# Attention by pairs of heads and modulation slabs by pairs, in a two-layer diffusion block

## The reference

```python
mod = silu(c) @ w_mod[layer] + b_mod[layer]        # 6 x 1024; the same for the context with c_ctx
hx = modulate(rms_norm(x, norm1_g), sh1, sc1)      # hc likewise
mx, mc = token_mixers(hx @ w_in, hc @ w_in, ...)   # GQA with 8 heads over 2 key heads, neighbourhood
                                                   # attention with 4 heads, pooling; gates, output projection
x = x + g1 * mx
hx = modulate(rms_norm(x, norm2_g), sh2, sc2)
x = x + g2 * (swiglu(h) if layer == 0 else moe_swiglu(hx))   # dense, then 2 of 8 experts
```

## Time and profile before

| stage | from | to |
|---|---|---|
| start: eight slabs, norm | 0 | 51.7 |
| projection, layer 0 | 51.7 | 155.5 |
| attention, pooling, layer 0 | 155.5 | 342.2 |
| merge, output projection, norm | 342.2 | 599.4 |
| feed-forward, norm of layer 1 | 599.4 | 1019.8 |
| projection, layer 1 | 1019.8 | 1100.0 |
| attention, pooling, layer 1 | 1100.0 | 1163.5 |
| merge, output projection, norm, router | 1163.5 | 1334.1 |
| experts, last norm | 1334.1 | 2379.4 |

### The profile page before, as it was taken

One profiled execution on the slowest core, in us unless ns is written; L12 is line 12 of the kernel. 1 busy time (PEld: TensorE's weight loads), 2 busy tenths in 40 slices (PEclk: granted clock), 3 DMA queues, 4 the chain that ended last, 5 costly groups with the idle time before them and its releaser, 6 DMA issues.

```text
span 2379.4 us, 27429 instructions
## 1 busy us (share of the span) xinstructions
PE 2286.7 (96%) x10670; PEld 1646.3 (69%) x10671; DVE 1159.3 (49%) x1372; ACT 1053.5 (44%) x1148; POOL 1287.2 (54%) x464
## 2 busy tenths in 40 slices
PE   6999999999999999899999899999999999999996
PEld 3875457664677878777797667677777777676774
DVE  3133421123101010335522687787878787878775
ACT  3222232202321222243431477666666666766664
POOL 2300013301443445440240599989898998898994
PEclk8999999999999999989999799999999999999998
DMA  7313442122233322231144699999999999999992
GB/s 279 109 54 124 148 173 89 71 89 106 89 136 141 109 93 80 80 124 36 56 193 158 266 364 344 348 341 350 340 345 344 352 357 336 352 342 347 347 346 101
DMA packets 69642, 503.17 MB, mean 211 GB/s; under 512 B 7744, under 2 KB 7872, under 8 KB 9088
## 3 DMA queue, kind: packets, MB, share of 16 engines
q1 hardware_dynamic: 68976, 497.91, 56.1%
q0 software_dynamic: 528, 3.41, 0.4%
HBM read 500.24 MB, written 1.05 MB: 211 GB/s over the span
## 4 chain that ended last, share of the span: by engine, by line
PE 50%; POOL 34%; issue 11%; ACT 2%; DVE 1%; DMA 1%; POOLq 0%; ACTq 0%; DVEq 0%; SPq 0%
POOL moe_lo L443 33%; PE bank L702 14%; PE bank L687 10%; PE bank L689 9%; PE bank L688 9%; PE pv_bank L702 2%; PE bank L853 2%; PE turned L872 1%; ACT H_NEW L1250 1%; DMA slab<-in_w_mod 1%; PE bank L857 1%; DMA moe_slab<-in_moe_up 0%; DVE SQ_SUM L1627 0%; PE bank L800 0%; POOL w_lo L413 0%
## 5 line engine op out<-in xcount | busy, mean ns | idle before, releaser
L443 POOL TENSOR_TENSOR moe_lo<-moe_slab,moe_hi 128x512 fp32r<-128x512 f32 x336 | 921.8, 2769 | 180.4 <-ACT moe_hi L1437 179.0
L443 DVE TENSOR_TENSOR moe_lo<-moe_slab,moe_hi 128x1536 fp32r<-128x1536 f32 x336 | 692.3, 2065 | 177.6 <-ACT moe_hi L1437 175.1
L413 POOL TENSOR_TENSOR w_lo<-slab,w_hi 128x2048 fp32r<-128x2048 f32 (+2 forms) x72 | 304.1, 4225 | 802.4 <-ACT w_hi L1214 802.3
L1437 ACT ACTIVATE moe_hi<-moe_slab 128x2048 fp32r<-128x2048 f32 x336 | 629.2, 1906 | 0.0
L687 PE MATMUL bank<-moe_hi,HE_HI 128*96 128x512 f32 x896 | 361.1, 403 | 9.0 <-issue 5.3
L689 PE MATMUL bank<-moe_hi,HE_LO 128*96 128x512 f32 x896 | 353.9, 395 | 0.0
L688 PE MATMUL bank<-moe_lo,HE_HI 128*96 128x512 f32 x896 | 352.7, 394 | 0.0
L687 PE MATMUL bank<-H_HI,w_hi 128*128 128x512 f32 (+1 forms) x880 | 326.5, 371 | 15.5 <-POOL H_LO L599 14.9
L688 PE MATMUL bank<-H_LO,w_hi 128*128 128x512 f32 (+1 forms) x880 | 319.8, 363 | 0.0
L689 PE MATMUL bank<-H_HI,w_lo 128*128 128x512 f32 (+1 forms) x880 | 319.6, 363 | 0.0
L1214 ACT ACTIVATE w_hi<-slab 128x2048 fp32r<-128x2048 f32 (+1 forms) x72 | 135.5, 1884 | 173.6 <-PE bank L689 114.0
(11 more groups left out here) (190 smaller groups left out, 2530.8 us busy)
## 6 DMA issues: line engine op xcount, KB each, us to landing
moe_slab<-in_moe_up SPq DMA_DIRECT2D x224, 1024.0 KB, 4.8
moe_slab<-in_moe_w SPq DMA_DIRECT2D x112, 1024.0 KB, 4.9
slab<-in_w_mod SPq DMA_DIRECT2D x48, 1024.0 KB, 4.8
slab<-in_w_in SPq DMA_DIRECT2D x38, 1024.0 KB, 4.8
slab<-in_ffn_w SPq DMA_DIRECT2D x30, 1024.0 KB, 4.8
slab<-in_w_proj SPq DMA_DIRECT2D x8, 1024.0 KB, 6.9
slab<-in_w_out SPq DMA_DIRECT2D x8, 1024.0 KB, 4.8
slab<-in_ffn_w SPq DMA_DIRECT2D x4, 768.0 KB, 4.2
```

The lines of the kernel that those rows point to most:

```text
L413: engine.tensor_tensor(lo, raw, hi.bitcast(F32), ALU.subtract).then_inc(done, 1)
L443: engine.tensor_tensor(moe_lo[n][:, blocks, :], moe_slab[k % MOE_RING][:, blocks, :], moe_hi[n][:, blocks, :].bitcast(F32), ALU.subtract). ...
L1437: af(moe_hi[k % MOE_SPLIT][:], moe_slab[k % MOE_RING][:], ACT.Copy).then_inc(moe_hi_ready, 1)
```

## The change

Heads go in pairs: a pair is the two heads that share a chunk of Y. Their scores are issued alternately from the two halves of the partitions of QK (or BQ), to different banks; their values go to the two halves of `pv_bank`, which ScalarE copies once for both. PT holds four heads' transposed probabilities instead of two. Latent and context pairs alternate in layer 0. TensorE's order is scores of the next pair (first query half), turn of head 0, values of the pair before, scores (second half), a pair of slabs, turn of head 1.

Slabs go in pairs: the sixteen matmuls of two slabs go in turn to four groups of 32 output partitions, the even and the odd eighths of the sum for each of two slabs. VectorE copies all 128 partitions. `turned_mod`, after two pairs, is four matmuls against a constant `fold` (128 x 4) that add the two halves of the sum and bring features to partitions. Pairs 0 to 3 (slabs 0 to 7) stand at the start, 4 to 15 in layer 0's attention, 16 to 21 (slabs 32 to 43) in layer 1's attention, 22 and 23 in the last norm. The second norm of layer 0, the feed-forward and the first norm of layer 1 have none.

```diff
@@ lists
-MOD_AT_START, MOD_IN_ATTENTION, MOD_IN_FFN = range(8), range(8, 32), range(34, 42)
-
-MOD_IN_NORM = {(0, 1): (), (0, 2): (32, 33), (1, 1): (42, 43), (1, 2): (44, 45, 46, 47)}
+MOD_PAIRS = 24
+MOD_AT_START = range(4)
...
+def attention_pairs(layer):
+    streams = (LAT, CTX) if layer == 0 else (LAT,)
+    return [(b, j, s) for b, n in (("A", 4), ("B", 2)) for j in range(n) for s in streams]
...
-    return [(b, h, s) for b, n in (("A", 8), ("B", 4)) for s in streams for h in range(n)]
+    return [(b, j, g, s) for b, j, s in attention_pairs(layer) for g in range(2)]
+MOD_IN_ATTENTION = (range(4, 16), range(16, 22))
+MOD_IN_NORM = (22, 23)
@@ TensorE
-            def mod(n):
...
-                filled(chain(out[32 * q:32 * q + 32, 0:256],
-                             [(small["cond"][:, 32 * k:32 * k + 32], w[:, k, :]) for k in range(DC)]), ("mod", n))
-                if q == 3:
-                    key = ("turned_mod", n // 4)
-                    out = fill(key)
-                    if n == 3:
-                        pe.wait_ge(consts_in, 16)
-                    for back in range(4):
-                        wait_taken(pe, ("mod", n - back))
+            def mod(i):
+                w, out = [slab(("mod", 2 * i + n))[0] for n in range(2)], fill(("mod", i))
+                for k in range(DC):
+                    for n in range(2):
+                        q = 2 * n + k % 2
+                        ins = mm(out[32 * q:32 * q + 32, 0:256], small["cond"][:, 32 * k:32 * k + 32], w[n][:, k, :],
+                                 start=k < 2, stop=k >= DC - 2)
+                filled(ins, ("mod", i))
+            def turned_mod(g):
+                out = fill(("turned_mod", g))
+                if g == 0:
+                    pe.wait_ge(consts_in, 16)
+                for q in range(2):
+                    wait_taken(pe, ("mod", 2 * g + q))
                     for m in range(2):
-                        ins = nc.tensor.transpose(out[:, P * m:P * m + P], small["modrow"][:, P * m:P * m + P], ident)
-                    filled(ins, key)
+                        row = 512 * (g % 2) + 256 * q + P * m
+                        ins = mm(out[:, 8 * q + 4 * m:8 * q + 4 * m + 4], small["modrow"][:, row:row + P], const("fold"),
+                                 start=True, stop=True)
+                filled(ins, ("turned_mod", g))
@@ TensorE, attention
+                    outs = [fill(("score", layer, 2 * p + g, t)) for g in range(2)]
+                        for g in range(2):
+                            lhs = q[half[g], c_lat + P * t:c_lat + P * t + P]
+                            filled(mm(outs[g][:], lhs, keys[g][half[g], :], start=True, stop=True),
+                                   ("score", layer, 2 * p + g, t))
...
-                    ins = chain(pv_bank[p0:p0 + HD, 0:S],
-                                [(V[:, t, vcol:vcol + HD], PT[:, u % 2, t, :]) for t in range(tiles)])
+                    for t in range(tiles):
+                        for g in range(2):
+                            ins = mm(pv_bank[HD * g:HD * g + HD, 0:S], V[:, t, cols[g]:cols[g] + HD],
+                                     PT[:, (2 * p + g) % 4, t, :], start=t == 0, stop=t == tiles - 1)
                     ins.then_inc(pv_full[layer], 1)
 
-                scores(0)
-                scores(1)
-                for u in range(len(units)):
-                    if u + 2 < len(units):
-                        scores(u + 2)
-                    if u:
-                        values(u - 1)
-                    turn(u)
-                    if layer == 0:
-                        mod(MOD_IN_ATTENTION[u])
-                values(len(units) - 1)
+                scores(0, 0)
+                scores(0, 1)
+                for p in range(len(pairs)):
+                    if p and p % 2 == 0:
+                        turned_mod(MOD_IN_ATTENTION[layer][p - 1] // 2)
+                    scores(p + 1, 0)
+                    turn(2 * p)
+                    if p:
+                        values(p - 1)
+                    scores(p + 1, 1)
+                    mod(MOD_IN_ATTENTION[layer][p])
+                    turn(2 * p + 1)
+                values(len(pairs) - 1)
+                turned_mod(MOD_IN_ATTENTION[layer][-1] // 2)
@@ ScalarE, attention
+                for p in range(len(pairs)):
+                    exps(2 * p + 1)
+                    turned_out(2 * p)
+                    if p:
+                        result(p - 1)
+                    if p + 1 < len(pairs):
+                        exps(2 * p + 2)
+                    turned_out(2 * p + 1)
@@ VectorE
+            def mod(i):
+                row = 256 * (i % 4)
+                wait_full(dve, ("mod", i))
...
@@ VectorE, attention
+                for p in range(pairs):
+                    normalise(2 * p)
+                    normalise(2 * p + 1)
+                    turned_out(2 * p)
+                    if p and p % 2 == 0:
+                        turned_mod(mods[p - 1] // 2)
+                    if p + 1 < pairs:
+                        maxima(2 * p + 2)
+                    mod(mods[p])
+                    turned_out(2 * p + 1)
+                    if p + 1 < pairs:
+                        maxima(2 * p + 3)
```

More of the change, by code:

```diff
@@ L113, in norm @@
             slabs.extend([("w1", 0, 0), ("w3", 0, 0)])
-        for n in MOD_IN_NORM[key]:
-            mod(n)
-    for n in MOD_AT_START:
-        mod(n)
+        if key == (1, 2):
+            for i in MOD_IN_NORM:
+                mod(i)
+            turned_mod(11)
+    for i in MOD_AT_START:
+        mod(i)
+        if i == 2:
+            turned_mod(0)
+    turned_mod(1)
     for layer in range(DEPTH):
@@ L130, in schedule, with scores @@
         fills.extend(("in", layer, ("u", m)) for m in range(layer, 2))
-        units = attention_units(layer)
-        for u in range(2):
-            fills.extend(("score", layer, u, q) for q in range(2 if units[u][2] == LAT else 1))
-        for u in range(len(units)):
-            if u + 2 < len(units):
-                fills.extend(("score", layer, u + 2, q) for q in range(2 if units[u + 2][2] == LAT else 1))
-            if layer == 0:
-                mod(MOD_IN_ATTENTION[u])
+        pairs = attention_pairs(layer)
+        def scores(p, t):
+            if p < len(pairs) and (pairs[p][2] == LAT or t == 0):
+                fills.extend(("score", layer, 2 * p + g, t) for g in range(2))
+        scores(0, 0)
[7 more added lines that the diff above has]
+        turned_mod(MOD_IN_ATTENTION[layer][-1] // 2)
         fills.extend(("pool", layer, p) for p in range(2))
@@ L156, in schedule @@
                     fills.extend([("w1", part, s, 0), ("w1", part, s, 1), ("w3", part, s, 0), ("w3", part, s, 1)])
-                    if later:
-                        mod(later.pop(0))
                 for j in range(4):
@@ L161, in schedule @@
                     fills.extend(("down", part, j, m) for m in range(2))
-                    if later:
-                        mod(later.pop(0))
-            assert not later
     fills.append(("logit",))
@@ L181, in last_fill @@
     if kind == "mod":
-        return slab
+        return ("mod", slab[1] // 2)
     if kind == "in":
@@ L874, in turn, with values @@
                     ins.then_inc(turned_full[layer], 1)
-                def values(u):
-                    branch, h, stream = units[u]
-                    _, p0, _, vcol, _ = place(branch, h)
-                    pe.wait_ge(turned_out_act[layer], u + 1)
-                    pe.wait_ge(turned_out_dve[layer], u + 1)
-                    if u == 0:
+                def values(p):
+                    branch, j, stream = pairs[p]
+                    cols = place(branch, j)[2]
+                    pe.wait_ge(turned_out_act[layer], 2 * p + 2)
+                    pe.wait_ge(turned_out_dve[layer], 2 * p + 2)
+                    if p == 0:
                         for name in (("av", 0), ("av", 1), ("bv", 0), ("bv", 1)):
@@ L1306, in attention @@
             def attention(layer):
[L1307 removed]
+                pairs = attention_pairs(layer)
                 def exps(u):
[L1310 removed]
+                    stream = pairs[u // 2][2]
                     act.wait_ge(nm_ready[layer], u + 1)
@@ L1635, in residuals @@
                         sum_squares(norm_key, *x_range(layer), c - 1)
-                    if c % 2 and later and norm_key != (layer, 2):
-                        mod(later.pop(0))
                 if norm_key:
@@ L1964, in expert @@
                     add_quarter(n, 4 * i + n + 1)
-            later = list(MOD_IN_FFN)
             v.memset(small["cond"][:], 0.0).then_inc(cond_zeroed, 1)
             dve.wait_ge(vecs_in, 16)
-            for n in MOD_AT_START:
-                if n == 4:
+            for i in MOD_AT_START:
+                if i == 2:
                     for c in range(1, DC):
                         sum_squares((0, 1), 0, T, c)
-                mod(n)
+                mod(i)
```

(3 more changed lines are left out.)

175 lines of the change are left out of this document (79 added, 96 removed).

## The result

The changed kernel takes 2307.8 us (median of 4 runs) beside 2380.5 us of the kernel before on the same chip: a ratio of 0.9691, 95% interval 0.9678 to 0.9703. It is faster by 73 us. The forecast was 2292, so the gain is 16 us short of it, inside the range. The profiled execution spans 2309.8 us, 17.9 above the 2291.9 of the sum. It is the slowest of the four; the fastest took 2302.7 us, at a mean granted clock of 0.966 instead of 0.959.

The account below looks back on a forecast made before the run. No single engine bounds the whole span; halving TensorE's work leaves a three-engine round trip pacing layer 0's attention. Terms +5.2 − 69.9 − 2.7 − 28.2 − 3.1 + 10.8 + 0.4 = −87.5 give 2292 us, range 2278 to 2320.

Parts of the forecast that it names:

- Side by side: TensorE in the attentions: slab pair 1.9 us in four streams, scores of two latent heads 2.0, values of two heads 1.9.
- Rivals 1, 2 and 4: Four column groups give two streams: 2321, chance 0.12; row halves run serially: 2312, 0.10; pairs run in series: 2393, 0.02.
- The round trip: Attentions, over three engines: latent plus context pair 17.7 us in layer 0, against 30.1 before; latent-latent pair 11.05 in layer 1.
- rival 5: TensorE's clock at the lower level all through both attentions: +122 us, 2414, slower than before; chance 0.05.
- The sign to look for: Granted clock dropping inside an attention would make the prediction wrong by tens of us.
- Feed-forward: Eight slabs and two turns of a row block taken out, less a newly exposed 2.85 us HID_LO wait: −28.2 us.
- Norms: Slabs taken out of layer 0's second norm and layer 1's first norm: −2.7 and −3.1 us.
- Start: Paired slabs with a ring of three, at half clock, delay the load ScalarE's second rounding waits for: +5.2 us.
- the bound with full clock: At the start, with the slab pairs at full clock, the delay would be below +1.8 us.
- Last norm: Pairs 22 and 23 before the router, whose products start earlier but run at half clock: +0.4 us (−2 to +2).

Follow-up runs that it names:

- the fillers: The changed kernel with filler products on TensorE ahead of each of the four slab pairs at the start: 2301.9 us.

## Why the prediction was right, and where it was off

**The number.** 2307.8 us lies 2 us above the forecast's own spread (2278 to 2306). It is inside the range because that had room up to 2320 for rivals that fell, so this part of the hit is luck. The gain itself came from where the prediction had put it.

**Side by side.** Right in all three. A slab pair is 1.93 us (I took 1.9), half scores of two heads 1.13 (1.0 to 1.05), values 1.95 (1.9). Rivals 1, 2 and 4 fall. For the pair I had set a rule beside the row: four column groups are 2 × 3.64/1.93 = 3.8 times as fast as one here, not 3.07 times, the figure that the Trainium skill gives for four row groups (TensorE: Matmul & The Clock Gate, Measured speedup vs the span model). The measurement decides.

**The round trip.** Right: 17.2 us at full clock for 17.7, and 11.0 for 11.05. At full clock the first attention to the merge is 113.5 us (107.6 + 5.9) against 116.8, the second 72.8 (69.4 + 3.4) against 74.3. VectorE's and ScalarE's hand-overs were not the miss.

**The clock: the term left out.** I had it as rival 5, at half clock all through the attentions or not at all, and argued that a TensorE busy three quarters of the time would keep it. It was busy 80 and 76% and had the lower level for 26 and 30% of the time; each of the 11 stretches begins in a wait of 1.9 to 4.1 us or in the first 2 us behind one. The sign to look for was named, a granted clock that drops inside an attention, at tens of us. The cost is 12.5 us in the first attention and 9.8 in the second (79.15 − 69.35), 22 us; the round trips were 5 better than counted. That is the 17.5 us by which the two attentions missed. The sum should have had this term as a part, not as a catastrophe: 55 us at the low level by 0.4. That price stood in rival 5 already, 17.7 us that become 30, so 12.3 us for 30 at the low level, or 0.41; what was missing was how much of the time it would be. The Trainium skill describes the like of it, a kernel in which TensorE "micro-idles" between groups of matmuls often enough for its clock to go back and forth (same page, A second HAM failure mode: psum-queue depth-cycling). This trace agrees, with low stretches of 3.4 to 6.8 us in the two attentions, though what TensorE waits for here is ScalarE and VectorE.

**Feed-forward.** −25.8 for −28.2. The wait for HID_LO at the end of the first part came as foreseen (3.19 us for 2.85), and behind it 3.4 us of low clock. Where the other 2 us went stays open. Norms: −2.6 and −4.0 for −2.7 and −3.1.

**Start.** +5.6 for +5.2. The pairs take 3.64, 3.64, 3.53 and 3.64 us for 3.5, nearly twice the 1.93 of full clock. (The clock record shows the lower level from 36.1 us on, so for the fourth pair; for the first three it has no entry, and their length alone says so.) ScalarE's second rounding starts at 46.5 instead of 40.5 us; the fillers reached +0.8 (52.45 us), a little under the bound with full clock, +1.8.

**Last norm.** −1.0 for +0.4, inside its bounds. The pairs are at half clock there, 3.64 and 3.50 us.

## What to carry to other kernels

When a packing halves an engine's work, write the round trip through all engines step by step, as it sets the pace from then on; then ask where in it the independent work stands. Ahead of the last step that another engine waits for, a slab pair of 1.93 us cost 1.0 to 1.2 us of every round trip of the first attention; behind that step it filled TensorE's own wait, and in the wait ahead of the down products it cost nothing. And count each wait of TensorE of some 2 us in such a loop as a risk to its clock: here 0.4 us for each microsecond that the lower level lasted, which idle products in the wait gave back.

## What the runs showed of the hardware beyond that

- Four groups of 32 output columns run fully side by side (float32, 256 columns): the four instructions of a step start within 0.02 us, and the next four 0.22 to 0.24 us behind.
- Products in different groups of 32 columns overlap even when one group's stand in front of the other's in the program: four instructions deep, as pairs of 1.93, 2.82 and 4.59 us for the same 32 instructions show.
- The granted clock did not follow how busy TensorE was over a stage. Two first attentions with TensorE busy 86% had 30.7 us at the lower level (scores from one row half, waits of 1.93 us and more) and 3.4 us (slab pair behind the second turn, waits of 1.16 us in its middle). A stage with 32 us more work and the same waits had the same 30.7 us, though of 152.5 us instead of 120.1. Against the same kernel's scatter, 27.3 to 30.7 in the first attention and 17.1 to 23.9 in the second, only large differences count. What exactly the chip looks at stays open: waits of 1.94 us were followed by a fall in some round trips and not in others.
- Products with the same 64 rows, and different banks, don't overlap: 1.98 us for four, 1.13 from two row halves.
